# Attention jobs of a two-block transformer kernel: segments of the window, differential, retention and cross heads in another order

## The reference

```python
# first block
h = rmsnorm(x, g);  dq, dk, dv, rq, rk, rv, rg = split(h @ w_in)
# 4 differential heads: two causal maps with ALiBi, a = softmax(s0) - lam * softmax(s1); rmsnorm(a @ v) * 0.2
# 4 retention heads: (q k^T * decay) v in two chunks; rmsnorm(...) * silu(rg)
x = x + concat(da, ret) @ w_o
# 4 cross heads of 512 columns over mem: softmax(hx_q k^T / sqrt(512)) v
x = x + xattn @ w_xo
x = x + (silu(hf @ w_gate) * (hf @ w_up)) @ w_down;  x = rmsnorm(x)
# second block
h = rmsnorm(x) * (1 + scale(c)) + shift(c)
# 8 window heads (2 groups of 4 query heads with one k, v): band of +-128 keys, relative bias, sink logit
y_a = window(q, k, v) * silu(gate_a);  y_p = multiscale_pool(u) * silu(gate_p)
out = x + gate(c) * rmsnorm((sigmoid(merge_a) * (y_a @ w_br_attn) + sigmoid(merge_p) * (y_p @ w_br_pool)) @ w_out)
```

## Time and profile before

| | us |
|---|---|
| median of 3 runs | 2135.74 (2135.18 to 2137.28) |
| the profiled execution | 2136.82 |
| its span, first to last instruction | 2135.0 |
| PE, DVE, ACT busy | 2075.8, 1678.9, 1173.1 |
| mean granted TensorE clock | 0.992 |

### The profile page before, as it was taken

How to read it: one execution, slowest core, us unless ns; L and a number is a source line. 1 busy time by engine, 2 the same in 40 slices (tenths; PEclk the granted TensorE clock), 3 DMA queues, 4 the chain that set the end, 5 groups by cost and what they waited for, 6 DMA issues and landing times.

```text
span 2135.0 us, 25372 instructions
## 1 busy us (share of the span) xinstructions
PE 2075.8 (97%) x9334; PEld 1705.4 (80%) x9334; DVE 1678.9 (79%) x1839; ACT 1173.1 (55%) x1519; POOL 72.5 (3%) x94
## 2 busy tenths in 40 slices
PE   8999999999999999999999999999899999999998
PEld 7877888778887888888888888887677788888786
DVE  6777778867666688989989988897687767998775
ACT  6555656665554566555555555555555554554453
POOL 1000001000000000000000000000310000000000
PEclk9999999999999999999999999999999999999999
DMA  9455557556553458777777777785465566889753
GB/s 337 158 161 170 178 167 236 176 198 198 187 178 128 146 180 290 235 248 262 258 228 244 266 247 239 238 275 196 129 198 177 158 194 198 289 274 323 230 197 108
DMA packets 218955, 453.75 MB, mean 213 GB/s; under 512 B 14400, under 2 KB 16592, under 8 KB 218704
## 3 DMA queue, kind: packets, MB, share of 16 engines
q1 hardware_dynamic: 212928, 432.07, 61.6%
q0 software_dynamic: 5616, 19.94, 2.9%
q10 hardware_dynamic: 288, 0.13, 0.0%
HBM read 447.88 MB, written 4.19 MB: 212 GB/s over the span
## 4 chain that ended last, share of the span: by engine, by line
PE 80%; DVE 8%; issue 8%; ACT 3%; DMA 2%; POOL 0%; SPq 0%; DVEq 0%; ACTq 0%; POOLq 0%
PE ps L1056 25%; PE ps L1058 25%; PE ps L1057 25%; DVE wlo L2276 3%; PE ps L648 2%; ACT whi L1568 1%; PE ps L779 1%; DMA raw<-in_w_in_dram 1%; DVE raw L2289 1%; PE ps L800 1%; DMA FR<-in_x_t_dram 1%; DMA FR<-in_mem_dram 0%; PE ps L916 0%; PE ps L905 0%; POOL Z L2328 0%
## 5 line engine op out<-in xcount | busy, mean ns | idle before, releaser
L2276 DVE TENSOR_TENSOR wlo<-raw,whi 128x1024 fp32r<-128x1024 f32 x832 | 1006.6, 1222 | 283.4 <-ACT whi L1568 277.2
L1568 ACT ACTIVATE whi<-raw 128x1024 fp32r<-128x1024 f32 x840 | 881.7, 1057 | 584.8 <-PE ps L1058 537.5
L1056 PE MATMUL ps<-whi,ah 128*128 128x512 f32 x1618 | 646.6, 400 | 13.7 <-ACT side L1163 5.8
L1058 PE MATMUL ps<-whi,al 128*128 128x512 f32 x1618 | 633.5, 392 | 0.0
L1057 PE MATMUL ps<-wlo,ah 128*128 128x512 f32 x1618 | 632.4, 391 | 0.0
L1056 PEld LDWEIGHTS ps<-whi,ah 128*128 128x128 f32 x1618 | 305.6, 189 | 81.3 <-ACT side L1163 7.9
L1058 PEld LDWEIGHTS ps<-whi,al 128*128 128x128 f32 x1618 | 305.1, 189 | 65.2
L1057 PEld LDWEIGHTS ps<-wlo,ah 128*128 128x128 f32 x1618 | 305.8, 189 | 61.7 <-issue 0.2
L1056 PE MATMUL ps<-whi,bh 128*128 128x512 f32 x862 | 341.7, 396 | 8.8 <-DVE wlo L2276 7.2
L1058 PE MATMUL ps<-whi,bl 128*128 128x512 f32 x862 | 336.8, 391 | 0.0
L1057 PE MATMUL ps<-wlo,bh 128*128 128x512 f32 x862 | 336.3, 390 | 0.0
(11 more groups left out here) (235 smaller groups left out, 1343.9 us busy)
## 6 DMA issues: line engine op xcount, KB each, us to landing
raw<-in_w_in_dram SPq DMA_DIRECT2D x168, 512.0 KB, 4.5
raw<-in_w_ada_dram SPq DMA_DIRECT2D x96, 512.0 KB, 4.6
raw<-in_w_gate_dram SPq DMA_DIRECT2D x88, 512.0 KB, 4.9
raw<-in_w_up_dram SPq DMA_DIRECT2D x88, 512.0 KB, 5.2
raw<-in_w_down_dram SPq DMA_DIRECT2D x88, 512.0 KB, 5.1
raw<-in_w_merge_dram SPq DMA_DIRECT2D x64, 512.0 KB, 4.9
raw<-in_w_o_dram SPq DMA_DIRECT2D x32, 512.0 KB, 4.6
raw<-in_w_xk_dram SPq DMA_DIRECT2D x32, 512.0 KB, 4.4
```

The lines of the kernel that those rows point to most:

```text
L1056: e.matmul(o, xh[:, k, tokens], wh, start=first, stop=False, skip_group_check=more)
L1058: ins = e.matmul(o, xl[:, k, tokens], wh, start=False, skip_group_check=more, stop=kk == 1 and (st.end or st.form in READ))
L1568: done(e.activation(whi[:, n % HALVES, :], place(item), ACT.Copy), "hi")
L2276: done(e.tensor_tensor(wlo[:, n % HALVES, :], src, whi[:, n % HALVES, :].bitcast(F32), ALU.subtract), "lo")
```

## The change

- *Window groups*: `window_head` is cut in three functions on each engine, and `window_group` lays them over each other: the scores of head h+1 are issued in the segment of the transposes of head h, the first transposes two segments after the first scores. A group takes 12 segments, before it took 14.
- *Differential heads*: ACT's exponentials and DVE's weights each move one segment later (1 and 2); all others stay.
- *Retention pairs*: both means are made ahead of the wait for the gate panel.
- *Cross heads*: the last one gets the same segments as the others, one more step between scores and transposes.
- *Forms of xo*: queued behind cross head 1, no longer behind cross head 0.

The number of instructions of each kind is the same, and so is the stream.

```diff
# PE
-                if h < 3:
-                    yield
+                yield
                 yield
                 e.wait_ge(s["c_p"], h + 1)
...
             def window_group(g):
                 for b in range(2):
                     e.wait_ge(T[b].free, T[b].n(f"q3{g}"))
+                window_scores(g, 0)
+                yield
+                yield
                 for hl in range(4):
-                    yield from window_head(g, hl)
+                    if hl < 3:
+                        window_scores(g, hl + 1)
+                    turn_window(g, hl)
+                    yield
+                    window_values(g, hl)
+                    yield
...
                     jobs.start(cross_head(i, p))
-                    if i == 0:
+                    if i == 1:
                         jobs.start(make_forms())
# ACT
             def diff_head(h):
+                yield
                 for i in range(2):
                     for q, sl in ((0, slice(0, 128)), (1, slice(128, 384))):
...
                 yield
                 yield
-                yield
                 e.wait_ge(T[0].full, T[0].n(f"aa{h}"))
...
             def window_group(g):
+                yield
+                window_exp(4 * g)
+                yield
                 for hl in range(4):
-                    yield from window_head(4 * g + hl)
+                    yield
+                    copy_window(4 * g + hl)
+                    if hl < 3:
+                        window_exp(4 * g + hl + 1)
+                    yield
# DVE
                 yield
+                yield
                 e.wait_ge(s["d_exp"], 4 * (h + 1))
...
                 done(ins, "d_aa")
                 yield
                 yield
-                yield
                 e.wait_ge(s["d_sq"], 2 * (h + 1))
...
                 yield
+                for i in range(2):
+                    e.wait_ge(s["e_sq"], 4 * pr + 2 * i + 2)
+                    mean(f"e{2 * pr + i}", ss_e[2 * pr + i], 2, 256)
                 wait_gate(index["rg", pr], 0, 1)
                 for i in range(2):
                     root = f"e{2 * pr + i}"
-                    e.wait_ge(s["e_sq"], 4 * pr + 2 * i + 2)
-                    mean(root, ss_e[2 * pr + i], 2, 256)
                     e.wait_ge(s["r"], root_n(root))
...
                 done(ins, "c_p")
-                yield
-                yield
+                for _ in range(2 if h < 3 else 3):
+                    yield
...
             def window_group(g):
                 wait_gate(index["ga", g], 0, 1)
+                window_logits(g, 0)
+                yield
+                yield
                 for hl in range(4):
-                    yield from window_head(g, hl)
+                    if hl < 3:
+                        window_logits(g, hl + 1)
+                    if hl:
+                        window_result(g, hl - 1, root)
+                    root = window_total(4 * g + hl)
+                    yield
+                    if hl == 3:
+                        window_result(g, hl, root)
+                    yield
```

More of the change, by code:

```diff
@@ L706, in diff_head @@
                              stop=True).then_inc(A[i].full, 1)
-                yield
-                yield
-                yield
+                for _ in range(3):
+                    yield
                 e.wait_ge(s["d_aa"], h + 1)
@@ L860, in turn_q3, with window_scores @@
                 yield from to_stationary(f"q3{g}", TQ3)
-            def window_head(g, hl):
+            def window_scores(g, hl):
                 h = 4 * g + hl
@@ L868, in window_head, with turn_window @@
                 ins.then_inc(A[0].full, 1)
-                yield
+            def turn_window(g, hl):
+                h = 4 * g + hl
                 e.wait_ge(s["w_exp"], 3 * h + 2)
@@ L876, in window_head, with window_values @@
                 ins.then_inc(T[0].full, 1)
-                yield
+            def window_values(g, hl):
+                h = 4 * g + hl
                 e.wait_ge(T[0].free, T[0].n(f"p3{h}"))
@@ L1407, in turn_q3, with window_exp @@
                 yield
-            def window_head(h):
+            def window_exp(h):
                 hl = h % 4
@@ L1415, in window_head, with copy_window, window_group @@
                 done(e.activation(w_es[h], w_nm2[h], ACT.Exp, bias=sink[:, h:h + 1]), "w_exp")
-                yield
+            def copy_window(h):
                 e.wait_ge(T[0].full, T[0].n(f"p3{h}"))
                 e.activation(PT3.rearrange("p a b -> p (a b)"), T[0].ap[:, :], ACT.Copy).then_inc(T[0].free, 1)
+            def window_group(g):
                 yield
+                window_exp(4 * g)
                 yield
-            def window_group(g):
                 for hl in range(4):
-                    yield from window_head(4 * g + hl)
+                    yield
[3 more added lines that the diff above has]
+                    yield
                 yield from to_stationary(f"ya{g}", ("ya", g))
@@ L2063, in turn_q3, with window_logits @@
                 yield
-            def window_head(g, hl):
+            def window_logits(g, hl):
                 h = 4 * g + hl
@@ L2074, in window_head, with window_total, window_result @@
                 done(e.tensor_scalar(w_nm2[h], w_nm[h], nsink[:, h:h + 1], None, ALU.min), "w_nm")
-                yield
+            def window_total(h):
                 e.wait_ge(s["w_exp"], 3 * h + 3)
                 after_own(done(e.tensor_tensor(w_tot[h], w_rs[h], w_es[h], ALU.add)))
-                root = done(e.reciprocal(w_rr[h], w_tot[h]))
-                yield
+                return done(e.reciprocal(w_rr[h], w_tot[h]))
+            def window_result(g, hl, root):
+                h = 4 * g + hl
                 e.wait_ge(A[1].full, A[1].n(f"wv{h}"))
```

## The result

The kernel after the change takes 2124.81 us (median of 4 runs, 2123.0 to 2124.99), the kernel before 2135.48 (4 runs, 2135.18 to 2137.28): a ratio of 0.9946, 95% interval 0.9929 to 0.9964. The two medians are 10.7 us or 0.5% apart. Predicted were 2122 and a range of 2116 to 2129. The profiled run took 2124.93 us with a span of 2123.1; against the profiled execution before the span is 11.9 us shorter.

The account below looks back on a forecast made before the run. PE, busy 97% of 2135.0 us, was taken as the bound, with time won only where it stands still or runs slow. Gains of 7.6 + 1.0 + 2.0 + 2.3 + 1.1 = 14.0 us gave 2122 us, range 2116 to 2129.

Parts of the forecast that it names:

- Windows, 7.6 predicted: Window groups: eight PE waits worth 8.2 us go, 0.3 us a group lost to a late copy; bounds 4 and 8.2.
- rival F: Window groups: table load also costs a 1.38 us drain, making head 0 1.0 us late in each; 2124 us; chance 0.03.
- Differential heads, 2.0 predicted: Differential heads: snapshot wait and slow clock go, new waits for weights come; net gain 2.0 us, bounds -2 and 6.
- allowance of 1.3: Differential heads: 1.3 us together set aside for slow clock behind new waits of 2.4 and 2.1 us.
- Cross head 1 and the forms, 2.3 predicted: Cross head 1: 6.4 us lost before, 3.8 after; gain 2.6, taken as 2.3; bounds -1 and 5.
- DVE's squeeze behind it: Cross heads 1 to 2: forms leave DVE little room before the xq2 panel ends; 0.5 us lost.
- Retention 1.0 predicted: Retention pairs: DVE earlier by about 0.7 and 0.4 us, PE waits less; gain 1.0 us, bounds 0 and 1.2.
- last cross head, 1.1 predicted: Cross head 3: one more step covers most of its wait before the transposes; gain 1.1 us, bounds 0 and 1.6.
- Rival B: Differential heads, cross head 1: new waits replace removed ones; windows keep 2 us of waits a group; 2130 to 2127; chance 0.25.
- C: Whole kernel: PE stays bound by DVE's low parts, each removed wait returns at the next step; 2135 us; chance 0.05.
- D: Slower: ACT holds copy and next exponentials in one segment, late maxima make casts stop PE; 2140 us; chance 0.03.
- rival E: Whole change: predicted mechanism without new slow clock and with cross head 1 less late; 2117 us; chance 0.12.

Follow-up runs that it names:

- heads alone: Kernel before with only the differential heads' exponentials (ACT) and weights (DVE) one segment later: 2135.96 us, ratio 1.0001.
- forms alone: Kernel before with only the forms of xo moved behind cross head 1: 2134.82 us, ratio 0.9996.
- windows alone: Kernel before with only the new window groups: 2125.11 us, ratio 0.9953.
- weights_back: Changed kernel with DVE's differential-head weights back where they were, ACT's exponentials still one segment later: 2117.13 us, ratio 0.9912 to the kernel before.
- warm-up run: Changed kernel with 26 instead of 18 warming matmuls ahead of the first step: 2120.99 us, one run.
- cross head 1 joined: Changed kernel with cross head 1's maxima and weights in one segment on DVE: 2119.51 us, one run.
- means alone: Kernel before with only both retention means ahead of the gate's wait and the last cross head's additional step: 2134.67 us, ratio 0.9995.
- last kernel with both edits: Changed kernel with differential weights back where they were and cross head 1's maxima and weights in one DVE segment: 2113.87 us, ratio 0.9897 to the kernel before.

## Why the prediction was right, and where its terms were off

The mechanism held part by part; the sum came out 14.0 predicted against 11.9 between the two profiled spans. That the sum is this close is in part luck: windows and retention brought 1.8 us more than predicted, the other three 2.8 less, and stretches that no edit touches took 1.1. Five terms:

- **Windows, 7.6 predicted, 8.9 measured.** The part alone repeats it (8.88), and both lie above the upper bound of 8.2. All eight waits that I counted went. By the starts of the matmuls around them, their idle time was 7.1 us (6.9 predicted) and the slower start behind them 2.2 (1.3 predicted): some 0.2 us behind six of them, 0.45 behind the two where PE stopped twice. The copy of a head's transposes, set at 0.3 us a group, made no wait. Against that the snapshot wait at the end of group 0, which I had left as it was, grew from 0.52 to 0.99. 7.1 + 2.2 - 0.5 = 8.8. That transposes and the next head's scores now lie in one segment saves nothing: without a wait they delay the stream by 1.3 us together (1617.70 to 1619.46, less two intervals of the stream), and by 0.86 and 0.45 apart. After (timeline of group 0, ACT and PE):

```profile
1608.10 1.05 ACT L1583 ACTIVATE whi<-raw 128x1024 fp32r<-128x1024 f32 x1
1609.17 1.28 ACT L1422 ACT_TABLE_LOAD   x1
1610.47 0.51 ACT L1422 ACTIVATE FR<-FR,Z 128x256 f32<-128x256 f32 x1
...
1615.58 0.51 ACT L1422 ACTIVATE FR<-FR,Z 128x256 f32<-128x256 f32 x1 [1.45 <-DVE Z L2090]
...
1617.93 1.02 PE L864 MATMUL ps<-FR 128*128 128x256 f32 x4
1618.79 0.38 PE L874 MATMUL ps<-ident,FR 128*128 128x128 f32 x2
```

  Head 1's exponentials start at 1615.58 and are two of 0.5 us, its transposes start at 1618.79 without a wait. The group begins 3.0 us earlier than I reckoned with; on that clock the prediction had the exponentials through by 1617.2 and the transposes due at 1618.9.
- **Table load, rival F.** The cast ends at 1609.15, the load starts at 1609.17 and ends at 1610.45, the exponentials start at 1610.47: 0.02 us on either side, now with the load in head 0's chain. The rule that I weighed (the Trainium skill, ScalarE: Activation LUTs, What ACT_TABLE_LOAD costs: 1.28 us and a drain of 1.38) agrees in the load's own length and not in the drain: no time stands beside it here. Rival F fell.
- **Differential heads, 2.0 predicted, 0.3 measured.** By the table: snapshot wait and its slow clock -4.35 (predicted -4.3); head 2 -0.64 and, for the slow stretch that stays away, -1.61 (predicted -0.4 and -1.7); head 3 +0.49 (predicted +0.65). Head 1's new wait cost 3.0 with its restart instead of 2.5 (as heads alone show with no slow clock in it, a step of +3.04), because the weights ended at 122.2 and not 121.6: the five low parts and two sums took 8.5 us (111.89 to 120.41) where I reckoned 8.0. The larger part is the allowance of 1.3 for the new waits' slow clocks: one of 6.7 us came, 2.8 us in all (3.29 + 2.53 - 3.04). These two, 0.5 and 1.5, are the terms that were off in size.
- **Cross head 1 and the forms, 2.3 predicted, 1.3 measured.** The chain of 4.94 us from scores to weights less two half steps gave 2.5 predicted, 2.4 measured with the restart, and DVE's squeeze behind it gave 0.6 for 0.5. The slow clock behind the wait (3.3 us at half speed) cost 1.5 where I allowed 0.8: the step of -1.32 against -2.84 in forms alone, which had none. And what was lost before was 5.8 us and not 6.4: its slow clock was worth 3.0 (windows alone) and not 3.3, and another 0.3 of my sum was not there. 5.8 - 2.4 - 0.6 - 1.5 = 1.3. The copy of head 1 is before 648, the scores run at 648.90 without a wait.
- **Retention 1.0 predicted, 1.5 measured** (0.96 and 0.56), and **last cross head, 1.1 predicted, 1.0 measured.** The two releases came forward by more than the 0.7 and 0.4 that I took, so the upper bound of 1.2 was itself too low.

A sixth amount was in no term: 1.1 us lost where no edit reaches (0.2 at the start, 0.6 with the half clock at 428, 0.3 before the window groups). Rival B, that the new waits take the place of the old in the differential and cross heads, was right by half: the waits exchange nearly 1 for 1 there, and both parts run alone can't be told from no change. It was wrong for the windows. With the windows whole it gave 2126, nearer to the measured 2124.8 than my 2122: the total does not choose between us, the shifts do. C and D fell: no cast was late in the window groups. What the change left was not a limit of the engines. With two steps moved the same program runs in 2113.87 us, so rival E's time (2117) was within reach through the order. Of the 10.6 us between it and the change in the two stretches, 6.0 are rows of waits and 4.3 the half clock that stood behind them.

The weights_back run also names which half of "a step apart" was the mistake: exponentials a step later free the snapshot and its cast; weights a step later put another low part of DVE ahead of them, and paid for it on PE three times.

Open stays why a given wait is followed by half clock and another of the same length is not. The warm-up run and the one with cross head 1 joined show that a wait's length alone does not decide, no more.

## What to carry to other kernels

Lay the next job's matmuls over this job's latency only where the engine that finishes the chain (here DVE) is left in front of its own stream work: count what is queued ahead of the last operation of the chain, on each engine, before moving it. A step pays where a whole job of another head lies between scores and transposes (windows, 8.9 us), not where it only exchanges one wait for another (differential heads, 0.3). Read a small gain by following the same instruction through both traces, because the total contains half-clock stretches that no edit made.

## What was not expected of the hardware

Waits of PE of 1.9 to 2.8 us are followed by half clock (1.2 GHz) or are not, for the same code. The longest waits at such places, by their rows in the timeline, and what followed in the profiled executions:

```
wait, us  place                         followed by half clock of
2.7       cross head 1, scores          6.8 us (before), none (windows alone), 3.4 (heads alone, means alone)
2.8       differential head 1           6.8 us (after), none (heads alone, warm-up 26), 3.4 (head 1 joined)
1.9       differential head 2           none (after, heads alone), 3.4 (warm-up 26, head 1 joined)
2.2       cross head 1, transposes      3.4 us (after, weights back, warm-up 26), none (forms alone)
2.1       window group 1                none (before, means alone), 3.4 (heads alone, forms alone)
```

A stretch cost somewhat less than half its length: 1.5 to 1.7 us for 3.4, 2.8 to 3.1 for 6.8. Such stretches are one reason why the same instructions took 2132.3 to 2140.6 us over 25 runs: the granted clock averaged 0.996 in the run of 2132.85 and 0.991 in that of 2139.87. Waits at the start of the kernel differ too (3.9 us before and 5.0 after at the same place near 50 us). Of an edit worth 2 us ten runs can show little; the trace's shifts show it at once. And removing a wait can be worth more than its length: without the waits for the weights and for cross head 1, the last kernel with both edits gained 10.6 us on the change in these two stretches, of which the waits' rows account for 6.0.
